# Seven-product up projection: one bank begun by a copy, two adds per pair on VectorE, taps that read banks, high parts by ScalarE

## The reference

```python
def conv_ffn(xn, ffn_up, ffn_conv_w, ffn_conv_b, ffn_down):
    u = causal_depthwise_conv(xn @ ffn_up, ffn_conv_w, ffn_conv_b)   # width 3 over tokens
    gate, up = jnp.split(u, 2, axis=-1)
    return (jax.nn.gelu(gate, approximate=True) * up) @ ffn_down
```

## Time and profile before

| what | value |
|---|---|
| median of 3 runs | 3135.95 us (3131.41 to 3137.43) |
| the profiled execution | 3138.06 us, span 3136.3 us |
| mean granted clock of TensorE | 0.960 |
| busy share | PE 92%, PEld 77%, DVE 60%, POOL 47%, ACT 37% |
| up projection, second token half | 691.9 to 1258.4 us |

### The profile page before, as it was taken

One profiled execution on the slowest core, in us unless ns is written; L12 is line 12 of the kernel. 1 busy time (PEld: TensorE's weight loads), 2 busy tenths in 40 slices (PEclk: granted clock), 3 DMA queues, 4 the chain that ended last, 5 costly groups with the idle time before them and its releaser, 6 DMA issues.

```text
span 3136.3 us, 42933 instructions
## 1 busy us (share of the span) xinstructions
PE 2890.1 (92%) x15236; PEld 2418.9 (77%) x15236; DVE 1866.7 (60%) x3188; ACT 1168.6 (37%) x2125; POOL 1466.0 (47%) x971
## 2 busy tenths in 40 slices
PE   7999998987888888999999999999999987889999
PEld 6689767776666666888888877998788885778887
DVE  3799838257666666331306567994203857978861
ACT  3311266242111111131312255773322445767750
POOL 2233133648777777766325434343433435323335
PEclk9999998899888888999999999999999998999999
DMA  4123341431111211644386625133433855121124
GB/s 143 60 96 127 100 101 31 148 114 43 61 60 60 73 41 34 222 122 140 122 157 203 202 60 147 41 94 108 146 141 127 247 151 125 50 75 34 45 98 139
DMA packets 224369, 336.29 MB, mean 107 GB/s; under 512 B 81910, under 2 KB 152438, under 8 KB 223686
## 3 DMA queue, kind: packets, MB, share of 16 engines
q1 hardware_dynamic: 200790, 289.88, 31.0%
q10 hardware_dynamic: 22192, 39.98, 3.5%
q0 software_dynamic: 1216, 4.20, 0.5%
HBM read 235.20 MB, written 98.81 MB: 106 GB/s over the span
## 4 chain that ended last, share of the span: by engine, by line
PE 74%; DVE 11%; issue 5%; POOL 4%; ACT 2%; DMA 2%; SPq 1%; DVEq 0%; POOLq 0%; ACTq 0%; PEldq 0%
PE psum L737 15%; PE psum L2568 8%; PE psum L3268 8%; PE psum L2934 7%; PE psum L444 6%; PE psum L1275 4%; PE psum L1306 3%; PE psum L1286 3%; PE psum L530 3%; PE psum L1573 2%; DVE arena L3077 2%; PE psum L984 2%; POOL parts_ffn L2820 2%; PE psum L962 1%; PE psum L973 1%
## 5 line engine op out<-in xcount | busy, mean ns | idle before, releaser
L2934 PE MATMUL psum<-up_t,parts_ffn 128*128 128x512 f32 x720 | 220.0, 463 | 91.7 <-DVE arena L3100 83.9
L737 PE MATMUL psum<-parts_even,parts_ffn 128*128 128x512 f32 (+1 forms) x1344 | 288.5, 376 | 0.0
L2934 PE MATMUL psum<-parts_ffn 128*128 128x512 f32 x1152 | 280.1, 397 | 8.6 <-POOL parts_ffn L2820 4.9
L737 PE MATMUL psum<-parts_odd 128*128 128x496 f32 (+1 forms) x1344 | 270.1, 361 | 7.3 <-POOL parts_odd L652 6.5
L737 PEld LDWEIGHTS psum<-parts_even,parts_ffn 128*128 128x128 f32 x1344 | 239.4, 189 | 44.7
L2934 PEld LDWEIGHTS psum<-up_t,parts_ffn 128*128 128x128 f32 x720 | 161.9, 228 | 140.1 <-DVE arena L3100 92.0
L2934 PEld LDWEIGHTS psum<-parts_ffn 128*128 128x128 f32 x1152 | 222.4, 193 | 59.5 <-POOL parts_ffn L2820 5.2
L737 PEld LDWEIGHTS psum<-parts_odd 128*128 128x128 f32 x1344 | 227.5, 192 | 42.9 <-POOL parts_odd L652 6.7
L444 PE MATMUL psum<-parts_mixer 128*128 128x512 f32 x912 | 210.0, 391 | 0.3 <-DVE parts_mixer L287 0.3
L444 PEld LDWEIGHTS psum<-parts_mixer 128*128 128x128 f32 x912 | 170.5, 188 | 35.8 <-DVE parts_mixer L287 0.5
L3100 DVE TENSOR_TENSOR arena<-psum,arena 128x512 f32<-128x512 f32 x100 | 66.8, 683 | 187.0 <-PE psum L2934 187.0
(11 more groups left out here) (424 smaller groups left out, 6664.6 us busy)
## 6 DMA issues: line engine op xcount, KB each, us to landing
arena<-ffn_down_k SPq DMA_DIRECT2D x44, 512.0 KB, 3.7
arena<-x SPq DMA_DIRECT2D x8, 2048.0 KB, 9.3
x<-arena SPq DMA_DIRECT2D x24, 512.0 KB, 3.8
arena<-w_in_e SPq DMA_DIRECT2D x24, 512.0 KB, 4.7
e_tokens<-arena ACTq DMA_DIRECT2D x24, 512.0 KB, 3.2
arena<-w_in_o SPq DMA_DIRECT2D x24, 496.0 KB, 5.9
arena<-ffn_up_b SPq DMA_DIRECT2D x11, 1024.0 KB, 5.8
up_raw_two<-ffn_up_b SPq DMA_DIRECT2D x11, 1024.0 KB, 5.7
```

The lines of the kernel that those rows point to most:

```text
L737: last = pe.matmul(self.bank(t, n), self.hT[:, a, k, t * P:(t + 1) * P], w, start=(k, a, b) == (0, 0, 0), stop=(k, a) == (KT - 1, 1))
L2934: last = pe.matmul(self.core.psum[:, bank, :], slot[:, a, k, :], operand[b][:, k, :], start=opens and (k, a, b) == (0, 0, 0), stop=(k, a) ...
```

## The change

Three pairs are plain now (`PLAIN = 3`), 19 take seven products. The order of the seven is a11 b11, S1 T1, S2 T2, a12 b21, S3 T3, S4 b22, a22 T4 (m0 to m6).

- **One bank begun by a copy.** ScalarE's `seed` copies bank 0 (m0 alone) into bank 2; T2's, T3's and T4's products then accumulate there, and b21's accumulates in bank 0.
- **Two adds.** ScalarE's `keep` copies bank 1 (T1's) and bank 2 (after T2's) to SBUF. VectorE's `join` adds the first to bank 2 (after T3's) and writes bank 3; later it adds the second to bank 1 (after b22's), in place.
- **Taps read banks.** A pair's sums are now its four banks, for every pair; `gate_sums` and `up_sums` go away, and TensorE waits for the taps of pair i - 2 (`conved`) before it takes the banks for pair i.
- **High parts by ScalarE.** From the fourth quarter of pair 3 on ScalarE writes the high parts and GpSimd the low parts alone. The whole corners and their sums, which GpSimd shared, are all formed by VectorE.
- The down projection's first block waits for the taps, and two of its weight buffers change places in its ring of three.

```diff
-    SLOTS = 4
+    SLOTS, PLAIN = 4, 3
...
     def banks_out(self, t):
-        j = self.tiles - 2
-        if t < 2:
-            return [(self.act_out, 2 * (j - 1)), (self.dve_out, 5 * (j - 1))]
-        return [(self.act_out, 2 * j), (self.dve_out, 5 * j)]
+        return [(self.conved, 2 * self.tiles - 2 if t < 2 else 2 * self.tiles)]
...
     def split(self, pool, i, m):
+        n, raw, high, low = self.place(i, m)
+        if n < self.by_pool:
+            self.ready(pool, i, m, n)
+            pool.tensor_copy(high, raw).then_inc(self.high_ready, 1)
+            pool.wait_ge(self.high_ready, n + 1)
+        else:
+            pool.wait_ge(self.scalar_high, n - self.by_pool + 1)
         pool.tensor_tensor(low, raw, high.bitcast(F32), ALU.subtract).then_inc(self.low_ready, 1)
...
     def gpsimd(self, pool):
-        for m in range(4):
-            weights.split(pool, 0, m)
-        hold(pool, self.second_half)
-        self.whole(pool, 1, 1).then_inc(self.full_pool, 1)
...
+        for i in range(self.tiles):
+            for m in range(4 if i < weights.PLAIN else 7):
                 weights.split(pool, i, m)
...
     def tensor(self, pe):
+        for i in range(plain, self.tiles):
+            j, n, at = i - plain, weights.first(i), 4 * (i % 2)
+            pe.wait_ge(self.conved, 2 * (i - 1))
+            self.product(pe, at, n, b11, True)
+            if i == plain:
+                pe.wait_ge(self.t_low, 4)
+            self.product(pe, at + 1, n + 1, t1, True)
+            pe.wait_ge(self.act_out, 3 * j + 1)
+            self.product(pe, at + 2, n + 2, t2, False)
+            self.product(pe, at, n + 3, b21, False)
+            pe.wait_ge(self.act_out, 3 * j + 3)
+            self.product(pe, at + 2, n + 4, t3, False)
+            self.product(pe, at + 1, n + 5, b22, False)
+            pe.wait_ge(self.dve_out, 2 * j + 1)
+            self.product(pe, at + 2, n + 6, t4, False)
...
+    def seed(self, act, i):
         self.formed(act, i, 0)
+        act.activation(self.bank(i, 2), self.bank(i, 0), ACT.Copy).then_inc(self.act_out, 1)
+
+    def keep(self, act, i, n):
+        j = i - self.weights.PLAIN
+        self.formed(act, i, n)
         if j:
+            act.wait_ge(self.dve_out, 2 * j - 2 + n)
+        act.activation(self.held[:, n - 1], self.bank(i, n), ACT.Copy).then_inc(self.act_out, 1)
...
     def scalar(self, act):
+        for i in range(plain, self.tiles):
             self.tap(act, i - 1, 1)
+            weights.high(act, i, 3)
+            self.seed(act, i)
+            weights.high(act, i, 4)
             self.gelu(act, i - 1)
+            self.keep(act, i, 1)
+            weights.high(act, i, 5)
+            self.keep(act, i, 2)
+            weights.high(act, i, 6)
...
+                for m in range(3):
+                    weights.high(act, i + 1, m)
             self.tap(act, i, 0)
...
+    def join(self, dve, i, n):
+        j = i - self.weights.PLAIN
+        if n == 0:
+            self.formed(dve, i, 4)
+            dve.wait_ge(self.act_out, 3 * j + 2)
+            dve.tensor_tensor(self.bank(i, 3), self.bank(i, 2), self.held[:, 0], ALU.add).then_inc(self.dve_out, 1)
+        else:
+            self.formed(dve, i, 5)
+            dve.wait_ge(self.act_out, 3 * j + 3)
+            dve.tensor_tensor(self.bank(i, 1), self.bank(i, 1), self.held[:, 1], ALU.add).then_inc(self.dve_out, 1)
...
     def vector(self, dve):
+        self.whole(dve, 0, 1).then_inc(self.formed_sums, 1)
+        self.whole(dve, 0, 0).then_inc(self.formed_sums, 1)
+        self.combine(dve, f11, f12, f11, 2)
+        self.whole(dve, 1, 1).then_inc(self.formed_sums, 1)
+        self.combine(dve, self.t2_full, f22, f11, 4)
         self.taps(dve, 0, 0)
         self.low(dve, 2, 0)
         self.taps(dve, 0, 1)
         self.gate(dve, 0)
+        self.combine(dve, f12, f22, f12, 5)
         self.low(dve, 3, 1)
+        self.whole(dve, 1, 0).then_inc(self.formed_sums, 1)
+        self.combine(dve, f21, f21, self.t2_full, 7)
+        self.low(dve, 4, 2)
+        self.taps(dve, 1, 0)
+        self.taps(dve, 1, 1)
+        self.gate(dve, 1)
+        weights.add_up(dve, plain)
+        self.low(dve, 1, 3)
+        for i in range(plain, self.tiles):
             self.taps(dve, i - 1, 0)
             self.taps(dve, i - 1, 1)
             self.gate(dve, i - 1)
+            if not last:
+                weights.add_up(dve, i + 1)
+            self.join(dve, i, 0)
...
+            self.join(dve, i, 1)
```

More of the change, by code:

```diff
@@ L2800, in add_up, with place, ready, high @@
         dve.tensor_tensor(s4, a12, s2, ALU.subtract).then_inc(self.summed, 1)
-    def sources(self, i):
+    def place(self, i, m):
+        n = self.first(i) + m
         a11, a12, a21, a22 = (self.quarter(i, f, k) for f in range(2) for k in range(2))
-        if i < 2:
-            return [a11, a12, a21, a22]
-        return [a11, self.sums[:, 0], a21, a12, self.sums[:, 1], self.sums[:, 2], a22]
-    def split(self, pool, i, m):
[L2809 to L2819, removed]
+        if i < self.PLAIN:
+            raw = (a11, a12, a21, a22)[m]
+        else:
+            raw = (a11, a21, self.sums[:, 0], a12, self.sums[:, 1], self.sums[:, 2], a22)[m]
+        slot = self.parts[:, n % self.SLOTS]
+        return [n, raw] + [slot[:, part].rearrange("p k f -> p (k f)") for part in range(2)]
+    def ready(self, engine, i, m, n):
+        if m == 0:
+            engine.wait_ge(self.loaded[i % 2], 16 * (i // 2 + 1))
+        if i >= self.PLAIN and m in (1, 2, 4, 5):
+            engine.wait_ge(self.summed, 4 * (i - self.PLAIN) + (0, 2, 3, 0, 4, 4)[m])
+        if n >= self.SLOTS:
+            engine.wait_ge(self.used, n - self.SLOTS + 1)
+    def high(self, act, i, m):
+        n, raw, high, _ = self.place(i, m)
+        self.ready(act, i, m, n)
+        act.activation(high, raw, ACT.Copy).then_inc(self.scalar_high, 1)
+    def split(self, pool, i, m):
+        n, raw, high, low = self.place(i, m)
[5 more added lines that the diff above has]
+            pool.wait_ge(self.scalar_high, n - self.by_pool + 1)
         pool.tensor_tensor(low, raw, high.bitcast(F32), ALU.subtract).then_inc(self.low_ready, 1)
@@ L2940, in tensor @@
     def tensor(self, pe):
-        weights = self.weights
+        weights, plain = self.weights, self.weights.PLAIN
         b11, b12, b21, b22 = ([self.corner(part, k, t) for part in range(2)] for k in range(2) for t in range(2))
@@ L2951, in tensor @@
             self.product(pe, 2 * s + 1, 2 * s + 1, b22, False)
[L2953 to L2958, removed]
-        t1, t2, t3, t4 = (self.t_parts(n) for n in (1, 2, 3, 4))
@@ L2960, in tensor @@
[L2960 to L2982, removed]
-                pe.wait_ge(self.t_low, 4)
-            pe.wait_ge(self.dve_out, 5 * j + 3)
-            self.product(pe, b, n + 6, t4, False)
+        for i in range(1, plain):
+            at, n = 4 * (i % 2), weights.first(i)
+            if i >= 2:
+                pe.wait_ge(self.conved, 2 * (i - 1))
+            if i == plain - 1:
+                self.product(pe, at + 1, n, b12, True, last_use=False)
+                self.product(pe, at + 3, n + 2, b12, True, last_use=False).then_inc(self.corner_free, 1)
+            for s in range(2):
+                self.product(pe, at + 2 * s, n + 2 * s, b11, True, last_use=i == plain - 1)
+                if i < plain - 1:
+                    self.product(pe, at + 2 * s + 1, n + 2 * s, b12, True)
+                self.product(pe, at + 2 * s, n + 2 * s + 1, b21, False, last_use=False)
+                self.product(pe, at + 2 * s + 1, n + 2 * s + 1, b22, False)
@@ L4586, in build @@
         aring = [core.take_parts(2, HALF) for _ in range(2)]
-        wring += [shaped(up.weights.parts[:, 2 * n:2 * n + 2].rearrange("p s a k f -> p (s a k f)"), (2, S)) for n in range(2)]
+        wring += [shaped(up.weights.parts[:, 2 * n:2 * n + 2].rearrange("p s a k f -> p (s a k f)"), (2, S)) for n in (1, 0)]
         core.top = held_at
```

115 lines of the change are left out of this document (36 added, 79 removed).

## The result

| | before | after |
|---|---|---|
| median (4 runs each, same chip) | 3134.2 us (3131.41 to 3137.43) | 2990.41 us (2986.25 to 2992.14) |
| profiled execution, span | 3138.06 us, 3136.3 us | 2990.36 us, 2988.6 us |
| mean granted clock | 0.960 | 0.979 |
| first up matmul to first down matmul | 671.4 to 1258.4: 587.0 us | 670.5 to 1113.0: 442.5 us |
| down projection | 242.8 us | 244.3 us |

The ratio after to before is 0.9539 (0.9522 to 0.9555): faster by 4.6%. The spans differ by 147.7 us: 144.5 less in the stage, 1.5 more in the down projection, and 4.7 less (0.9 ahead of the stage, 3.8 behind it) in stages whose code is the same in both kernels.

The account below looks back on a forecast made before the run. TensorE was held by T4's wait for the m4 join in VectorE's queue. 143.7 us saved, less 1.0 start, 1.9 end and 0.6 clock, is 140.2 net: 2997.9, less 2.1 to the median, 2996 us; range 2990 to 3006.

Parts of the forecast that it names:

- What bounds the kernel: Up projection: T4 waits 4.44 us for the m4 join, queued on VectorE behind taps, four weight sums and the gate.
- The walk through a pair: Queue times of one new seven-product pair: TensorE never waits, so a pair takes 19.38 us.
- The sum: Second token half 422.8 us against 566.5; net gain 140.2 us after small losses, giving 2996 us.
- The pair: Each of 19 seven-product pairs takes 19.38 us, 368.2 us together.
- The start: T1 of pair 3 waits for VectorE's whole corners: 1 us taken, 0 to 10.3 possible.
- The end: Down projection's third token tile waits 1.8 to 1.9 us for taps, then 0.6 us of slower clock.
- From the profiled execution to the median: Profiled execution of the kernel before lies 2.1 us above the timed median, so 2997.9 us becomes 2996.
- own range 2990 to 3006: Range around the 2996 us forecast, allowing a start of 0 to 10 us and a few tenths a product.
- The short wait before m6: Rival: late weight sums delay the first join, 19 to 48 us over 19 pairs, 3015 to 3044 us; chance 0.12.
- The clock: Rival: TensorE's clock stays at the mean 0.89 in the second half, 52 us more, 3048 us; chance 0.04.
- A seed slow enough to cost time: Slower rival: TensorE waits at m2 for ScalarE's seed; free below 2.5 us, 7.9 us loses all gain; chance 0.02.
- The down projection didn't give the gain back: No-effect rival: a late raw load sets the pair or the down projection returns the time, near 3136 us; chance 0.01.

Follow-up runs that it names:

- gate_behind_join: Kernel before, with VectorE's gate of the pair before moved behind the m4 join; 3074.02 us, ratio 0.9819.
- sums_behind_joins: Kernel before, with VectorE's four weight sums for the next pair moved behind both the m4 and m5 joins; 3032.3 us, ratio 0.969.
- sums_behind_highs_scalar: sums_behind_joins, with ScalarE instead of GpSimd making the high parts from the fourth quarter of pair 2 on; 3018.95 us, ratio 0.9637.
- seed_x7: Kernel after, with the seed's copy made seven times, each waiting for the last; 3022.6 us, ratio 0.965.

## Why the prediction came out as it did

**What bounds the kernel** was read rightly: the gate taken out from ahead of the m4 join shortened TensorE's wait by its own length (gate_behind_join), the sums by theirs less what the taps grew (sums_behind_joins), and with short waits the clock is 1.00. The pair of 25.46 us that the prediction read is the shortest of three that follow in turn (25.46, 26.28 and 26.77 us), as T4 takes 4.46, 5.30 and 5.49 us behind equal waits; the sum goes by the whole 566.5 us and is not touched by it.

**The walk through a pair** holds in its parts. Forecast and measured, from the pair's first matmul: sums begin at 8.36 and 8.2; they end at 13.64 and 12.2 (one of them lost a turn to GpSimd, where two were allowed); the first join starts at 14.03 and 14.0; its slack is 1.87 and 1.85; that of the seed 1.94 and 1.94. The copy of 512 columns that no row had showed 582 ns, near the 0.60 taken. By the formula of the Trainium skill, "ScalarE: Activation LUTs", section "What ACT_TABLE_LOAD costs", the estimate is 612 ns, and the measured 582 decides. The same page of the Trainium skill says in the section "Step-by-step: what each stage is for" that ScalarE writes to PSUM faster than to SBUF; 582 against the 599 of line 3036 agrees.

**The sum** failed in size only. The forecast lies 5.6 us above the median, and four terms of it were mis-sized, the first three by 2.8 us together:

- The pair: 19.34 us, not 19.38; the second half took 421.95 us for 422.8.
- The start: I took 1.0 us out of 0 to 10.3; it cost nothing. VectorE's timeline in the kernel after shows the last corner's low part:

```profile
740.88 3.38 DVE L3100 TENSOR_TENSOR parts_ffn<-arena,parts_ffn 128x2048 fp32r<-128x2048 f32 x1
```

It ends at 744.26, and T1 of pair 3 wants it at 691.03 + 54.6 + 2.75 = 748.4: 4.1 us to spare, where the walk left 1.3 to 2.3. VectorE took 53.2 us to get there, against 48.7 without interference and 55 to 56 in the walk, which counted more turns with GpSimd than were lost.

- The end: the gap is 1.63 us for 1.9, and the clock behind it stays at 1.00, so the 0.6 us for the clock was nothing (the product behind the gap of 2.50 us that it was read from had taken 3.04 us). The down projection grew by 1.5 us for 2.5.
- From the profiled execution to the median: the prediction took off the 2.1 us by which the profiled execution of the kernel before lies above the median of three runs. With the fourth run it lies 3.9 us above (3138.06 - 3134.2), while the kernel after's lies on its median: 1.8 us more. In the traces 4.7 us lie in stages that the change doesn't touch. There, the ten traces of kernels with the same code differ from each other: 648 to 653 us from the start of the axial attention to that of the differential one, 530 to 536 from there to the end.

So the step that failed is the size of these small terms, and the range that was laid around them. "I take 1 us and keep 0 and 10.3" for the start measured 0; 2.5 us for the end measured 1.5; 19.38 us a pair measured 19.34; the 2.1 us was 3.9. All four erred to the same side, by 4.6 us together; the last 1.0 is less than single runs of the kernel after differ by (5.9). "own range 2990 to 3006 (start from 0 to 10 us, and a few tenths a product)" left 10 us above the forecast and only 6 below, though the costs of the start and of the clock could well be nothing. No wait and no path was missed.

**The rivals.** The short wait before m6 didn't come: TensorE's wait is 0.0 for that group. The clock came back, 1.00 throughout, but the argument that the prediction held against this rival was wrong: that the down projection has a wait at each block and shows 1.00. The earlier trace rows show TensorE busy for all of 100.00 us there, and by the page of the kernel before it waited for 1.3 us in the whole down projection:

```profile
L3268 PE MATMUL psum<-parts_ffn 128*128 128x512 f32 x720 | 167.1, 389 | 1.3 <-POOL parts_ffn L3245 1.3
```

What speaks against the rival are the experiments: with waits of 4.44, 2.35 and 0.88 us a pair the clock is 0.88, 0.94 and 1.00. A seed slow enough to cost time needs over 2.5 us, and takes 0.58. The down projection didn't give the gain back.

**Where the 144.5 us come from**, by the stage of the kernels in the table: 99.2 for the sums behind the joins, 15.0 for ScalarE's high parts on top of that, 30.3 for the rest of the change. Of the 30.3, the pair's length gives 14.1 (20 x 20.17 = 403.4 against 19 x 19.34 and eight plain products of 2.73, 389.3); 7.5 are the two waits for GpSimd at the start (4.67 and 2.86 in sums_behind_highs_scalar), which are gone, and 1.5 the slow product behind the second. Another 5.5 stand at the last pair, as TensorE's timeline in sums_behind_highs_scalar shows:

```profile
713.64 23.69 PE L2952 MATMUL psum<-parts_ffn 128*128 128x512 f32 x96 [4.67 <-POOL parts_ffn L2838]
740.20 4.56 PE L2952 MATMUL psum<-up_t,parts_ffn 128*128 128x512 f32 x12 [2.86 <-POOL parts_ffn L2838]
...
1143.36 4.61 PE L2952 MATMUL psum<-up_t,parts_ffn 128*128 128x512 f32 x12 [4.49 <-DVE arena L3125]
```

In the last pair this kernel, like the kernel before, lets VectorE make two early splits for the down projection (4.28 us from 1138.43) ahead of the m4 join, so its T4 waits 4.49 us in place of 0.55 and runs slowly behind the wait; the change puts the first join ahead of these splits, and there is no wait. That is again a matter of the queue's order. Some 2 us were not taken apart. This split goes by one order of making the edits; the two experiments on the high parts show that another order would divide it otherwise. Two joins in place of five and the seed by themselves, in the old order of VectorE's queue, were not tried. Nor was the old data flow with gate, sums and early splits all behind the joins, so how much of the gain needs the new data flow at all is open.

## What to carry to other kernels

When an engine is half idle and another waits for it, look first at what stands ahead of the awaited instruction in its queue: moving one statement behind it gave two thirds of what a new data flow gave. An edit that takes work off a third engine is worth what the current bound makes of it: the same edit cost 17 us, gained 15 and did nothing in three kernels. When a sum is made of careful small costs, let the range reach to their being zero, and add what untouched stages vary by.

## What the hardware showed beside

- Equal waits were not followed by equal clocks: behind waits of 2.35 and 2.36 us, 15 T4 products took 4.37 to 4.61 us and three took 3.06 (gate_behind_join). Waits of 1.63 us before T2 in seed_x7 were never followed by a slow product (the group's mean is 397 ns), and a gap of 1.63 us in the down projection left the clock at 1.00. The Trainium skill, "TensorE: Matmul & The Clock Gate", section "A second HAM failure mode: psum-queue depth-cycling", warns of a clock that swings where a loop through banks idles a little; the kernel before and gate_behind_join show such a swing, seed_x7 doesn't.
- A tap with one input in PSUM doesn't slow down beside GpSimd, one with both in SBUF does. Single lines of the kernel after, durations in ns (min/median/max):

```profile
L3083 DVE SCALAR_TENSOR_TENSOR arena<-psum,arena x88: 1270/1282/1285, 704.0 to 1116.2; 128x1023 f32<-128x1023 f32 x44, 128x1022 f32<-128x1022 f32 x44
L3028 ACT ACTIVATE psum<-psum x19: 582/582/582, 748.5 to 1096.6; 128x512 f32<-128x512 f32 x19
L3108 DVE TENSOR_TENSOR psum<-psum,arena x19: 699/700/700, 759.5 to 1107.6; 128x512 f32<-128x512 f32 x19
```

All 88 taps lie within 15 ns, while the 80 taps out of SBUF in sums_behind_joins took 1.27 to 3.30 us, with a median of 2.12. The Trainium skill, "SBUF — State Buffer", section "Who interferes with whom", says that VectorE and GpSimd share a pair of ports, which is an exclusive lock; the traces agree with that, with 1.28 us a tap against a median of 2.12.
- A sum that VectorE writes into PSUM takes 700 ns against 679 into SBUF; ScalarE's copy goes the other way, 582 ns into PSUM and 599 into SBUF.
